# First norm of a two-layer trunk step: the modulation of channel blocks 4 and 5, and of 6 and 7, computed side by side

## The chip, the cores and the metric

The kernel runs on one core of a Trainium2 chip. The metric is the device time of one execution in microseconds (us). The kernel before took 1227.86 us, the median of three runs (1227.62 to 1229.47).

A core has five engines that run side by side, each through its own queue in order: TensorE (PE in the profile, with its weight loads as PEld), VectorE (DVE), ScalarE (ACT), GpSimd (POOL) and SyncE (SP), which here only issues DMA transfers. They wait for each other by semaphores. TensorE writes its results into PSUM, a memory of 8 banks, from which DVE and ACT read.

## The reference, cut to what matters

Two layers, run on 128 context tokens and 256 latent tokens, 1024 channels. Each layer begins with a norm whose scale and shift come from a conditioning vector by a matrix product (the "modulation"), and one wide input projection of the normed tokens:

```python
mod = jnp.einsum('bd,de->be', jax.nn.silu(cond), p['w_ada']) + p['b_ada']
sh1, sc1, g1, sh2, sc2, g2 = jnp.split(mod[:, None, :], 6, axis=-1)
h = _rms(x, p['g_norm1']) * (1 + sc1) + sh1
u = h @ p['w_in']
...
x = x + g1 * (merged @ p['w_out'])
h2 = _rms(x, p['g_norm2']) * (1 + sc2) + sh2
x = x + g2 * _conv_ffn(h2, p['w_up'], p['conv_w'], p['conv_b'], p['w_down'])
```

`_rms` divides by the root of the mean square over the channels. Between these lines stand four token mixers (pooling, differential attention, a Fourier transform, latent attention). The change touches only how `sh1`, `sc1` and the first part of `h @ p['w_in']` of layer 0 are put in order.

## The kernel before

Tokens lie along the free dimension (384 columns), channels along the 128 partitions, so the 1024 channels are 8 blocks (`KD = 8`), and a product of 128 output channels is a sum over 8 channel blocks. Each product is done in three matmuls of 128 x 384, with the weight and the activation each split into a high and a low part (high x high, high x low, low x high). ACT makes the high parts, DVE the low parts.

At the start of layer 0 everything is new: conditioning, modulation weights, tokens and projection weights arrive by DMA while the first norm is being computed. The kernel therefore goes block by block over the input channels. For channel block j there are these pieces of work, with their names in the code:

- **The loads** (SP, L473 and L475): `start_ada`, 1024 KB of modulation weights for block j, and `start_raw`, 448 KB of projection weights (seven output blocks of 128). SP issues them in the order of j, the two of a block one behind the other. There are six buffers for `start_ada` (`START_ADA = 6`), so those of blocks 6 and 7 are issued once the modulation of block 0 and of block 1 is done.
- **The modulation**, `start_modulate(j)` (PE, L1492), below **M j**: 32 small matmuls. The stationary operand is the conditioning vector padded to 32 columns, so each matmul fills 32 of the 128 columns of the array, in four strips; the result is 64 columns wide and lands in PSUM bank 7, in columns of its own for each block. In the profile a group of these has 64 records.
- **The norm**, `start_norm(j)` (DVE, L1066 to L1088): it waits until M j is done, reads it out of bank 7 with a transpose (L1066, which counts up the semaphore `start_read`), adds the bias (L1073), forms the scale (L1077), and scales the tokens (L1082, two instructions). It then makes the low part of the projection weights of this block (L1058, `start_low`), and, when ACT has made the high part of the normed block (`act_hi`, L658), the low part (L1088, two instructions).
- **ACT**, in its own order: the high part of the projection weights of block j (`start_hi`), then `act_hi` of block j, then `start_hi` of block j + 1.
- **The products**, `start_products(j)` (PE, L1503, L1507, L1508), below **P j**: 21 matmuls of 128 x 384 into banks 0 to 6, seven high x high first (L1503), then seven pairs of (high weight x low activation, L1507) and (low weight x high activation, L1508). P j waits for `start_hi` and `act_hi` of block j, and behind its first seven for the low parts.

PE's order in the kernel before is M0, M1, P0, M2, P1, M3, P2, M4, P3, M5, P4, M6, P5, M7, P6, P7: the modulation of block j + 2 stands between P j and P j + 1. Two semaphores keep PE and DVE apart in bank 7, which both use: M j waits until DVE has read the modulation of block j - 1 (`start_read >= j`, L1487), and DVE waits for M j as a whole (`ada_done >= 2 * (j + 1)`, L1065).

Behind P7 comes the first dense unit of the rest of the projection (L1435 to L1437), whose weights come through the general stream (`w_raw`, four slots), and then the rest of the layer. SP's queue behind the starting loads: four units of the stream, parameters, caches, constants; then two loads of modulation rows (`ada<-ada_rows`, L446), which wait for M7; then loads that wait for P7.

The loop that the change rewrites, and the two waits:

```python
if j >= 1:
    pe.wait_ge(start_read, j)
...
start_modulate(0)
start_modulate(1)
for j in range(KD):
    start_products(j)
    if j + 2 < KD:
        start_modulate(j + 2)
```

Of the kernel before, what the change touches and what calls it, by code (L numbers as in the profile page):

```python
# [25 lines left out]
KD = D // P  # L26
# [30 lines left out]
ADA = 48  # L57
HEAD = 16
START_ADA = 6
WARM = 11  # L60


# [110 lines left out]
def program(nc, stream, start_w, ada_w, ada_rows, start_ada, params, caches, consts, time_consts, x_in, cond,  # L173
            y_out, k_out, v_out, ckv_out, krope_out):
    ctx = ExitStack()
    with ctx:
        def tile(name, width, offset, dt=F32, parts=P):

            offset = -(-offset // 32) * 32
            return nc.alloc_sbuf_tensor_at(name, [parts, width], dt, offset=offset), offset + 4 * width  # L180

        def sem(name):
            return ctx.enter_context(nc.semaphore(name))
# [8 lines left out]
        late_t, _ = tile("gated_late", KD * TOK, o)  # L192
# [62 lines left out]
        brl_t, _ = tile("branch_lo", 8 * TOK, first_at, F32R)  # L255
# [12 lines left out]
        headb_t, _ = tile("ada_head_b", HOLE_LOW * UNIT, alo_at)  # L268
# [19 lines left out]
        start_ada_buf = [tile("start_ada0", 2 * UNIT, ada_at)[0]]  # L288
        o = rt_end - 4 * 2 * LAT - 4 * 2 * UNIT * (START_ADA - 1)
        assert o >= val_at  # L290
        for n in range(1, START_ADA):
            t, o = tile(f"start_ada{n}", 2 * UNIT, o)
# [40 lines left out]
        def pc(name, a=0, b=None, p0=0, p1=P):  # L333
            lo, hi = PCOL[name]
            return par[p0:p1, lo + a:(hi if b is None else lo + b)]

        def cc(name, p0=0, p1=P, a=0, b=None):
            lo, hi = CCOL[name]
            return cn[p0:p1, lo + a:(hi if b is None else lo + b)]
# [26 lines left out]
        shift_ready, gate2_ready = sem("shift_ready"), sem("gate2_ready")  # L366
        start_ada_loaded = [sem(f"start_ada_loaded{n}") for n in range(START_ADA)]
        start_w_loaded = [sem(f"start_w_loaded{j}") for j in range(KD)]
# [9 lines left out]
        hi_ready, lo_ready, unit_done, ada_done = sem("hi_ready"), sem("lo_ready"), sem("unit_done"), sem("ada_done")  # L378
# [37 lines left out]
        def _(sp):  # L416
# [53 lines left out]
            for j in range(KD):  # L470
                if j >= START_ADA:
                    sp.wait_ge(ada_done, 2 * (j - START_ADA + 1))
                sp.dma_start(start_ada_buf[j % START_ADA][:, :], start_ada[j:j + 1, :, :].rearrange("a p n -> (a p) n")  # L473
                             ).then_inc(start_ada_loaded[j % START_ADA], 16)
# [462 lines left out]
        def _(dve):  # L937
# [32 lines left out]
            for l in range(DEPTH):  # L970
# [84 lines left out]
                def start_low(j):  # L1055

                    dve.wait_ge(start_w_hi, j + 1)
                    V.tensor_tensor(start_lo[j][:, :], start_raw[j][:, :], start_hi[j][:, :].bitcast(F32), ALU.subtract  # L1058
                                    ).then_inc(start_w_lo, 1)

                def start_norm(j):

                    c0 = j * 2 * STRIP
                    turned_block = rt_t[:, c0:c0 + 2 * STRIP].rearrange("p (b c) -> p b c", c=STRIP)
                    dve.wait_ge(ada_done, 2 * (j + 1))  # L1065
                    turn = V.transpose(rt_t[:, c0:c0 + 2 * STRIP], bank[7][:, c0:c0 + 2 * STRIP])  # L1066
                    if j < KD - 1:
                        turn.then_inc(start_read, 1)
                        dve.wait_ge(start_read, j + 1)
                    else:  # L1070
                        turn.then_inc(mod_read, 2)
                        dve.wait_ge(mod_read, FROM + 2)
                    V.tensor_tensor(mod[:, j:2 * KD:KD, :], turned_block[:, :, 0:2],  # L1073
                                    pc("b_ada", 0, 2 * KD)[:, j:2 * KD:KD].unsqueeze(2).to_broadcast([P, 2, 2]), ALU.add
                                    ).then_inc(start_shift, 1)
                    dve.wait_ge(start_shift, j + 1)
                    own(V.scalar_tensor_tensor(sc1[:, j:j + 1, :], mod[:, KD + j:KD + j + 1, :], 1.0,  # L1077
                                               pc("g1", j, j + 1).unsqueeze(2).to_broadcast([P, 1, 2]), ALU.add, ALU.mult))
                    own.wait()
                    dve.wait_ge(rstd_ready, 1)  # L1080
                    for a, b, c in RANGES:
                        ins = V.scalar_tensor_tensor(wide[:, j, a:b], x[:, j, a:b], sc1[:, j, c:c + 1], rsn[:, a:b],  # L1082
                                                     ALU.mult, ALU.mult)
                    ins.then_inc(norm_full, 1)
                    start_low(j)
                    dve.wait_ge(norm_hi, j + 1)
                    for a, b, c in RANGES:
                        ins = V.scalar_tensor_tensor(alo[:, j, a:b], wide[:, j, a:b], mod[:, j, c:c + 1],  # L1088
                                                     ahi[:, j, a:b].bitcast(F32), ALU.add, ALU.subtract)
                    ins.then_inc(norm_lo, 1)  # L1090
# [293 lines left out]
        def _(pe):  # L1384
# [30 lines left out]
            def hole_units():  # L1415

                pe.wait_ge(mod_read, FROM + READ_AT[1, 3])
                for n in range(KD):
                    if n % 4 == 0:
                        pe.wait_ge(hole_ada_loaded[n // 4], 64)  # L1420
                    modulate(hole[n], HOLE_ADA + n)

            pe.wait_ge(ones_loaded, 16)
            for l in range(DEPTH):
# [47 lines left out]
                def start_squares():  # L1472

                    for _ in range(WARM):
                        T.matmul(bank[6][:, 0:P], cc("ones"), cc("ones"), start=True, stop=True)
                    for h in range(2):
                        pe.wait_ge(start_sq_sum, h + 1)
                        for k in (4 * h, 4 * h + 1):
                            ins = T.matmul(bank[4][:, 0:TOK], cc("ones"), wide[:, k, :], start=k == 0, stop=k == 5)
                    ins.then_inc(ss_done, 1)  # L1480

                def start_modulate(j):

                    w = start_ada_buf[j % START_ADA]
                    pe.wait_ge(start_ada_loaded[j % START_ADA], 16 * (j // START_ADA + 1))
                    if j >= 1:
                        pe.wait_ge(start_read, j)  # L1487
                    n = 2 * STRIP
                    for k in range(KD):
                        for strip in range(4):  # L1490
                            p0, c = STRIP * strip, (k * 4 + strip) * n
                            ins = T.matmul(bank[7][p0:p0 + STRIP, j * n:(j + 1) * n], conds[:, k, :], w[:, c:c + n],  # L1492
                                           start=k == 0, stop=k == KD - 1)
                    ins.then_inc(ada_done, 2)

                def start_products(j):

                    outs = [bank[u][:, 0:TOK] for u in range(SKIP)]
                    cols = [slice(u * P, (u + 1) * P) for u in range(SKIP)]
                    pe.wait_ge(start_w_hi, j + 1)  # L1500
                    pe.wait_ge(norm_hi, j + 1)
                    for u in range(SKIP):
                        T.matmul(outs[u], start_hi[j][:, cols[u]], HI[j], start=j == 0, stop=False)  # L1503
                    pe.wait_ge(start_w_lo, j + 1)
                    pe.wait_ge(norm_lo, j + 1)
                    for u in range(SKIP):
                        T.matmul(outs[u], start_hi[j][:, cols[u]], LO[j], start=False, stop=False)  # L1507
                        ins = T.matmul(outs[u], start_lo[j][:, cols[u]], HI[j], start=False, stop=j == KD - 1)  # L1508
                        if j == KD - 1:
                            ins.then_inc(unit_done, 1)  # L1510

                if l == 0:
                    start_squares()
                    pe.wait_ge(cond_ready, 1)
                    start_modulate(0)
                    start_modulate(1)
                    for j in range(KD):
                        start_products(j)
                        if j + 2 < KD:
                            start_modulate(j + 2)  # L1520
                else:
                    square_sums(0)
                    hole_units()
                    group(0, (0, 1, 2), HI, LO, lambda k: pe.wait_ge(norm_lo, l * 2 * KD + k + 1))
# [463 lines left out]
```

## Time and profile before

| | |
|---|---|
| median of 3 runs | 1227.86 us (1227.62 to 1229.47) |
| the profiled execution's own time | 1227.43 us |
| its span (first to last instruction) | 1225.5 us |
| PE busy in it | 1209.1 us (99%) |
| DVE, ACT, POOL busy | 909.8, 574.4, 140.4 us |
| mean granted clock of TensorE | 0.999 |
| DMA | 198.82 MB, 162 GB/s over the span |

A timeline row gives start, length, engine, line, operation, output and inputs; `x7` is the number of instructions drawn together in the row, and the bracket at its end is how long the engine had been idle and what ended that. Matmul records are longer than their spacing, since they are pipelined: what one costs is read from the starts. "us to landing" of a DMA counts from its issue.

### The profile page before, as it was taken

How to read it: one execution, taken by the hardware profiler on the slowest of the kernel's cores; microseconds unless marked ns; L12 is line 12 of the kernel's file. 1: busy time of each engine (PE TensorE's matmuls, PEld its weight loads, DVE VectorE, ACT ScalarE, POOL GpSimd, SP SyncE). 2: the span in 40 equal slices, each digit the busy share in tenths (PEclk: the TensorE clock that was granted, in tenths of full speed). 3: DMA queues.
4: the chain of work that ended last, by engine and by line, in shares of the span. 5: the costliest groups of instructions: out<-in, count | busy, mean ns of one | idle time of the engine just before them, and what ended most of it. 6: DMA issues, size and time to landing. Idle time of an engine off the chain costs nothing.

```text
span 1225.5 us, 19777 instructions
## 1 busy us (share of the span) xinstructions
PE 1209.1 (99%) x7816; PEld 1150.7 (94%) x7816; DVE 909.8 (74%) x1671; ACT 574.4 (47%) x949; POOL 140.4 (11%) x109
## 2 busy tenths in 40 slices
PE   7999999999999999999999999999999999999999
PEld 6987999989989999999989889999998999999998
DVE  5588877848679999987787865765596977877432
ACT  3445565543265445443354446656335654554321
POOL 0222000007310000000115210000281000000000
PEclk9999999999999999999999999999999999999999
DMA  9853333544644444459664522222245334334343
GB/s 371 323 182 123 137 121 116 171 143 155 237 176 146 165 155 166 153 191 345 217 238 169 187 81 101 93 100 99 99 165 206 121 121 134 125 122 137 132 142 122
DMA packets 53532, 198.82 MB, mean 162 GB/s; under 512 B 6784, under 2 KB 7200, under 8 KB 51904
## 3 DMA queue, kind: packets, MB, share of 16 engines
q1 hardware_dynamic: 53120, 196.86, 46.0%
q8 instruction: 63, 1.03, 0.3%
q0 software_dynamic: 320, 0.69, 0.1%
q14 instruction: 29, 0.24, 0.1%
HBM read 195.25 MB, written 2.27 MB: 161 GB/s over the span
## 4 chain that ended last, share of the span: by engine, by line
PE 91%; DVE 4%; issue 2%; DMA 2%; ACT 1%; SPq 0%; DVEq 0%; ACTq 0%
PE bank L1435 26%; PE bank L1437 26%; PE bank L1436 26%; PE bank L1734 1%; DVE w_lo L976 1%; DMA start_ada<-start_ada 1%; PE bank L1714 1%; PE bank L1503 1%; PE bank L1508 1%; PE bank L1704 1%; PE bank L1507 1%; ACT w_hi L658 1%; DVE gated_late L1295 1%; PE bank L1689 1%; PE bank L1492 1%
## 5 line engine op out<-in xcount | busy, mean ns | idle before, releaser
L1435 PE MATMUL bank<-act_hi,w_hi 128*128 128x384 f32 x1368 | 465.0, 340 | 0.7 <-DVE act_lo L1051 0.3
L1437 PE MATMUL bank<-act_hi,w_lo 128*128 128x384 f32 x1368 | 457.8, 335 | 0.0
L1436 PE MATMUL bank<-act_lo,w_hi 128*128 128x384 f32 x1336 | 446.6, 334 | 0.0
L976 DVE TENSOR_TENSOR w_lo<-w_raw,w_hi 128x1024 fp32r<-128x1024 f32 x251 | 318.3, 1270 | 117.8 <-ACT w_hi L658 117.2
L658 ACT ACTIVATE w_hi<-w_raw 128x1024 fp32r<-128x1024 f32 x251 | 264.2, 1053 | 165.1 <-DMA w_raw<-stream 165.0
L1435 PEld LDWEIGHTS bank<-act_hi,w_hi 128*128 128x128 f32 x1368 | 257.1, 188 | 10.7 <-issue 6.5
L1437 PEld LDWEIGHTS bank<-act_hi,w_lo 128*128 128x128 f32 x1368 | 256.8, 188 | 0.0
L1436 PEld LDWEIGHTS bank<-act_lo,w_hi 128*128 128x128 f32 x1336 | 251.0, 188 | 0.6
L1437 PE MATMUL bank<-mlp_hi,w_lo 128*128 128x384 f32 x352 | 118.3, 336 | 0.0
L1435 PE MATMUL bank<-mlp_hi,w_hi 128*128 128x384 f32 x352 | 118.3, 336 | 0.0
L1436 PE MATMUL bank<-mlp_lo,w_hi 128*128 128x384 f32 x352 | 118.3, 336 | 0.0
L1341 DVE SCALAR_TENSOR_TENSOR mlp_tmp<-bank,params,mlp_tmp 128x127 f32<-128x127 f32 (+1 forms) x176 | 64.7, 409 | 38.0 <-ACT mlp_tmp L658 38.0
L658 ACT ACTIVATE mlp_tmp<-bank,params 128x384 f32<-128x384 f32 x88 | 54.2, 667 | 81.3 <-PE bank L1437 81.3
L1345 DVE SCALAR_TENSOR_TENSOR mlp_tmp<-bank,params,mlp_tmp 128x127 f32<-128x127 f32 (+1 forms) x176 | 65.2, 412 | 3.1
L1437 PEld LDWEIGHTS bank<-mlp_hi,w_lo 128*128 128x128 f32 x352 | 66.2, 188 | 0.0
L1435 PEld LDWEIGHTS bank<-mlp_hi,w_hi 128*128 128x128 f32 x352 | 66.2, 188 | 0.0
L1436 PEld LDWEIGHTS bank<-mlp_lo,w_hi 128*128 128x128 f32 x352 | 66.2, 188 | 0.0
L1229 DVE TENSOR_REDUCE small<-bank 128x1 f32<-128x384 f32 (+1 forms) x72 | 31.3, 463 | 40.8 <-PE bank L1705 15.6
L1007 DVE SCALAR_TENSOR_TENSOR row_products<-ada,cond_spread 128x1024 f32<-128x1024 f32 x48 | 61.0, 1270 | 0.6 <-DMA ada<-ada_rows 0.4
L658 ACT ACTIVATE gates_b<-bank 128x384 f32<-128x384 f32 x48 | 23.6, 492 | 67.6 <-PE bank L1437 67.3
L1007 DVE SCALAR_TENSOR_TENSOR row_products_mix<-ada,cond_spread_mix 128x1024 f32<-128x1024 f32 x38 | 52.1, 1372 | 0.2
L649 POOL TENSOR_TENSOR wide<-wide 128x768 f32<-128x768 f32 x8 | 17.3, 2158 | 274.9 <-DVE wide L1295 274.9
(246 smaller groups left out, 1590.1 us busy)
## 6 DMA issues: line engine op xcount, KB each, us to landing
w_raw<-stream SPq DMA_DIRECT2D x251, 512.0 KB, 3.3
ada<-ada_rows SPq DMA_DIRECT2D x48, 512.0 KB, 4.3
start_ada<-start_ada SPq DMA_DIRECT2D x8, 1024.0 KB, 18.5
ada_norm<-ada_w SPq DMA_DIRECT2D x16, 512.0 KB, 5.9
ada<-ada_w SPq DMA_DIRECT2D x8, 512.0 KB, 5.5
start_raw<-start_w SPq DMA_DIRECT2D x8, 448.0 KB, 19.1
ada_head_a<-ada_w SPq DMA_DIRECT2D x5, 512.0 KB, 6.7
cond_spread_mix<-cond_rows SPq DMA_DIRECT2D x2, 1024.0 KB, 8.2
```

The lines of the kernel that those rows point to most:

```text
L649: own(nc.gpsimd.tensor_tensor(g[:, 0:2, :], g[:, 0:2, :], g[:, 2:4, :], ALU.add))
L658: return nc.scalar.activation(out, in_, func, **kw)
L976: V.tensor_tensor(wlo[s][:, :], raw[s][:, :], whi[s][:, :].bitcast(F32), ALU.subtract).then_inc(lo_ready, 1)
L1007: V.scalar_tensor_tensor(out[:, :], ada[b % 2][:, :], 1.0, tile[:, t, :], ALU.mult, ALU.mult, accum_out=mod[:, at, t:t + 1]).then_inc(rows ...
L1229: own(V.reduce_max(small[:, c + m:c + m + 1], bank[score_bank(i, m)][:, 0:n], AX))
L1295: V.scalar_tensor_tensor(gated[d % GATED][:, n, :], gates[n * KD + d], 1.0, bank[branch_bank[4 * d + n]][:, 0:TOK], ALU.add, ALU.mult).the ...
L1341: own(V.scalar_tensor_tensor(f[:, m, a + 1:e], b[:, a:e - 1], before, f[:, m, a + 1:e], ALU.mult, ALU.add))
L1345: ins = V.scalar_tensor_tensor(f[:, m, a:e - 1], b[:, a + 1:e], behind, f[:, m, a:e - 1], ALU.mult, ALU.add)
L1435: T.matmul(out, wb[s][0][:, w, :], hi[k], start=first and k == 0, stop=False)
L1436: T.matmul(out, wb[s][0][:, w, :], lo[k], start=False, stop=False)
L1437: ins = T.matmul(out, wb[s][1][:, w, :], hi[k], start=False, stop=last and k == n - 1)
L1492: ins = T.matmul(bank[7][p0:p0 + STRIP, j * n:(j + 1) * n], conds[:, k, :], w[:, c:c + n], start=k == 0, stop=k == KD - 1)
```

## The change

PE's loop is now driven by a table of groups. Blocks 1, 2 and 3 are groups of one, blocks 4 and 5 are one group, and 6 and 7 another. PE first makes the modulations of a group, and then the products of the blocks one before them. `START_LAST` gives for each block the last block of its group. M5 and M7 no longer wait for a read by DVE; DVE reads block 4 only when M5 is done too, and block 6 only when M7 is done, so that PE never writes to bank 7 while DVE reads it.

```diff
 START_ADA = 6
+START_GROUPS = ((0,), (1,), (2,), (3,), (4, 5), (6, 7))
+START_LAST = [group[-1] for group in START_GROUPS for _ in group]
...
-                    dve.wait_ge(ada_done, 2 * (j + 1))
+                    dve.wait_ge(ada_done, 2 * (START_LAST[j] + 1))
                     turn = V.transpose(rt_t[:, c0:c0 + 2 * STRIP], bank[7][:, c0:c0 + 2 * STRIP])
...
-                    if j >= 1:
+                    if j >= 1 and START_LAST[j - 1] != START_LAST[j]:
                         pe.wait_ge(start_read, j)
...
                     start_modulate(0)
-                    start_modulate(1)
-                    for j in range(KD):
-                        start_products(j)
-                        if j + 2 < KD:
-                            start_modulate(j + 2)
+                    for together in START_GROUPS[1:]:
+                        for j in together:
+                            start_modulate(j)
+                        for j in together:
+                            start_products(j - 1)
+                    start_products(KD - 1)
```

PE's order becomes M0, M1, P0, M2, P1, M3, P2, M4, M5, P3, P4, M6, M7, P5, P6, P7. The order of instructions on DVE, ACT, POOL and SP stays as it was.

This is PE's queue before, from the end of P2 to the begin of P4. The numbers are buffers: `start_ada_148` is block 4's modulation weights and `start_ada_149` block 5's; `start_hi_128`, `_131` and `_134` are the projection weights of blocks 2, 3 and 4.

```order
L1507 MATMUL bank<-act_lo,start_hi_128 128x384
L1508 MATMUL bank<-act_hi,start_lo_127 128x384
L1492 MATMUL bank<-start_ada_148,cond_silu 32x64 x32
L1503 MATMUL bank<-act_hi,start_hi_131 128x384 x7
...
L1507 MATMUL bank<-act_lo,start_hi_131 128x384
L1508 MATMUL bank<-act_hi,start_lo_130 128x384
L1492 MATMUL bank<-start_ada_149,cond_silu 32x64 x32
L1503 MATMUL bank<-act_hi,start_hi_134 128x384 x7
```

And the same stretch of the changed kernel (its lines are two higher here):

```order
L1509 MATMUL bank<-act_lo,start_hi_128 128x384
L1510 MATMUL bank<-act_hi,start_lo_127 128x384
L1494 MATMUL bank<-start_ada_148,cond_silu 32x64 x32
L1494 MATMUL bank<-start_ada_149,cond_silu 32x64 x32
L1505 MATMUL bank<-act_hi,start_hi_131 128x384 x7
...
L1509 MATMUL bank<-act_lo,start_hi_131 128x384
L1510 MATMUL bank<-act_hi,start_lo_130 128x384
L1505 MATMUL bank<-act_hi,start_hi_134 128x384 x7
```

M5 has moved ahead of the 21 matmuls of P3, and P4 follows P3 directly. The same happens around P5. Before, from the end of P4 to P6 (`start_ada_144` and `_145` are the buffers of blocks 6 and 7, `start_hi_137` and `_140` the weights of blocks 5 and 6):

```order
L1508 MATMUL bank<-act_hi,start_lo_133 128x384
L1492 MATMUL bank<-start_ada_144,cond_silu 32x64 x32
L1503 MATMUL bank<-act_hi,start_hi_137 128x384 x7
...
L1508 MATMUL bank<-act_hi,start_lo_136 128x384
L1492 MATMUL bank<-start_ada_145,cond_silu 32x64 x32
L1503 MATMUL bank<-act_hi,start_hi_140 128x384 x7
```

And in the changed kernel:

```order
L1510 MATMUL bank<-act_hi,start_lo_133 128x384
L1494 MATMUL bank<-start_ada_144,cond_silu 32x64 x32
L1494 MATMUL bank<-start_ada_145,cond_silu 32x64 x32
L1505 MATMUL bank<-act_hi,start_hi_137 128x384 x7
...
L1510 MATMUL bank<-act_hi,start_lo_136 128x384
L1505 MATMUL bank<-act_hi,start_hi_140 128x384 x7
```

M7 has moved ahead of P5, and P6 follows P5 directly. On PE two of the six places where a modulation stands between products are gone; on the other engines nothing moves, only what they wait for.

## Rows read from the trace of the kernel before

**Rows 1.** The page, busy time of each engine: us (share of the span) xinstructions.

```profile
PE 1209.1 (99%) x7816; PEld 1150.7 (94%) x7816; DVE 909.8 (74%) x1671; ACT 574.4 (47%) x949; POOL 140.4 (11%) x109
```

**Rows 2.** Waits of PE, whole span: waiting <- waited for: us, times, longest.

```profile
PE bank L1435 <- DVE w_lo L976: 2.7, 3, 2.0
PE bank L1557 <- ACT rstd L658: 2.5, 2, 2.2
PE bank L1492 <- DMA start_ada<-start_ada: 2.0, 2, 1.6
```

**Rows 3.** Timeline of PE: M1, M2, M4, P3, M5, P4, P6, P7, first dense unit.

```profile
14.86 1.10 PE L1492 MATMUL bank<-start_ada,cond_silu 128*32 128x64 f32 x64 [1.64 <-DMA start_ada<-start_ada]
20.19 1.10 PE L1492 MATMUL bank<-start_ada,cond_silu 128*32 128x64 f32 x64 [0.39 <-DMA start_ada<-start_ada]
29.96 1.10 PE L1492 MATMUL bank<-start_ada,cond_silu 128*32 128x64 f32 x64
30.99 1.48 PE L1503 MATMUL bank<-act_hi,start_hi 128*128 128x384 f32 x7
...
34.83 1.10 PE L1492 MATMUL bank<-start_ada,cond_silu 128*32 128x64 f32 x64
35.87 1.48 PE L1503 MATMUL bank<-act_hi,start_hi 128*128 128x384 f32 x7
...
45.61 1.48 PE L1503 MATMUL bank<-act_hi,start_hi 128*128 128x384 f32 x7
49.36 1.38 PE L1503 MATMUL bank<-act_hi,start_hi 128*128 128x384 f32 x7
53.00 0.34 PE L1435 MATMUL bank<-act_hi,w_hi 128*128 128x384 f32 x1
```

**Rows 4.** The modulations' matmuls, whole span: count, ns min/median/max, first and last start.

```profile
L1492 PE MATMUL bank<-start_ada,cond_silu x512: 219/219/243, 12.1 to 45.5; 128*32 128x64 f32 x171
```

**Rows 5.** Timeline of DVE and ACT, norm of block 4.

```profile
31.13 0.25 DVE L1066 STREAM_TRANSPOSE rope_tmp<-bank 128x64 f32<-128x64 f32 x1 [1.77 <-PE bank L1492]
32.47 1.08 DVE L1058 TENSOR_TENSOR start_lo<-start_raw,start_hi 128x896 fp32r<-128x896 f32 x1
32.65 0.80 ACT L658 ACTIVATE act_hi<-wide,mod 128x128 fp32r<-128x128 f32 x2 [3.23 <-DVE wide L1082]
33.49 0.75 DVE L1088 SCALAR_TENSOR_TENSOR act_lo<-wide,mod,act_hi 128x128 fp32r<-128x128 f32 x2
```

**Rows 6.** Loads of blocks 4, 5 and 7: issue on SP, then us to landing.

```profile
7.45 0.43 SPq L473 DMA_DIRECT2D start_ada<-start_ada  x1
8.40 0.84 SPq L473 DMA_DIRECT2D start_ada<-start_ada  x1
16.67 1.61 SPq L473 DMA_DIRECT2D start_ada<-start_ada  x1
start_ada<-start_ada SPq DMA_DIRECT2D x1, 1024.0 KB, 19.8
start_ada<-start_ada SPq DMA_DIRECT2D x1, 1024.0 KB, 22.4
start_ada<-start_ada SPq DMA_DIRECT2D x1, 1024.0 KB, 21.4
```

**Rows 7.** Timeline: the two row loads behind M7, and ACT's first stream units.

```profile
45.74 1.14 SPq L446 DMA_DIRECT2D ada<-ada_rows  x2
48.05 2.94 ACT L658 ACTIVATE w_hi<-w_raw 128x1024 fp32r<-128x1024 f32 x3
```

**Rows 8.** Timeline of ACT and PE between 64 and 74 us.

```profile
64.55 0.60 ACT L658 ACTIVATE val<-bank 128x512 f32<-128x512 f32 x1 [5.75 <-PE bank L1540]
73.33 0.61 PE L1557 MATMUL bank<-rstd,consts 32*128 32x384 f32 x4 [2.20 <-ACT rstd L658]
```

**Rows 9.** Stretches: us, busy (x) of PE, PEld, DVE, ACT, POOL, granted clock, DMA share, GB/s.

```profile
308.00:312.00 4.00, 2.14 (x10) 2.17 (x11) 4.00 (x6) 0.53 (x1) 2.85 (x3) 0.89 0.34 122
312.00:316.00 4.00, 4.00 (x17) 4.00 (x17) 4.00 (x3) 0.29 (x1) 3.60 (x2) 0.68 0.80 283
```

## The prediction

> **What bounds the kernel now.** I read the page first. PE is busy 99% of the span [rows 1], so a change counts only where it alters PE's time: an instruction less, a stall less or a wait more. Then the waits of PE alone [rows 2]: the largest are 2.7, 2.5 and 2.0 us, spread over the program, so there is no large wait to be won, and the third of them is the place of the change, the modulations that waited for their weights. Third, the timeline of PE in the first 53 us [rows 3]. The reader is to see where the loads pace PE and where they no longer do: M1 at 14.86 and M2 at 20.19 are released by a DMA; from then on no row of PE up to the first dense unit carries a bracket, so PE works through its queue without a visible wait. From M2 on this stretch is bound by PE itself, in steps of 34.83 - 29.96 = 4.87 us for one modulation and one block of products.
>
> **What a modulation between products costs.** P7 stands between two pieces of full-width work and takes 53.00 - 49.36 = 3.64 us. P6 comes from a modulation and goes into products: 49.36 - 45.61 = 3.75 us. P3 comes from a modulation and goes into one: 34.83 - 30.99 = 3.84 us [rows 3]. Entering products from a modulation thus costs 0.11 us, and leaving them for one 0.09. The modulation takes 30.99 - 29.96 = 1.03 us from its first matmul to the first product. But its group of 64 records is 1.10 us long and one record of it lasts 0.219 [rows 4], so the last one starts 0.88 us after the first; at that spacing (0.88 / 63 = 0.014) a following modulation could start after 0.89. The remaining 0.14 us is again the step from strips to full width. Put between products, a modulation has 0.20 + 0.14 = 0.34 us of such steps beside 0.89 of its own.
>
> **What the change removes.** M5 no longer stands between P3 and P4, nor M7 between P5 and P6. The same 32 matmuls run directly behind M4 and M6. No instruction is added or dropped. The boundary M4 to M5 (and M6 to M7) has no row in this trace. From below: it costs nothing, each pair saves 0.34 us, the two 0.68. From above: the boundary also carries a wait (for the weights), and if it pays the 0.14 us of the modulation's end and a new entry of 0.09, a pair saves 0.11, the two 0.22. Below nothing I exclude, since 0.89 us is already the bare spacing of the records. The nearest row of a boundary between like work is P6 to P7, whose waits are met and which costs nothing: P7 has the 3.64 us that 21 matmuls take at 0.173 each. I take nothing for the boundary: minus 0.68 us.
>
> [...]
>
> **What the change adds: waits.** There are three.
>
> First, M5 is reached earlier, at 29.96 + 0.89 = 30.85 us instead of 34.83, and needs the modulation weights of block 5. They were issued at 8.40 and landed 22.4 us later, at 30.80 [rows 6]. That is 0.05 us of slack where there were 4.03. In this execution the wait is zero; it is the one step of the change that hangs on a DMA, and it has a rival of its own below. For M7 the margin is wide: reached at about 40.25, its weights landed at 16.67 + 21.4 = 38.07; those of block 6 are ahead of them in the same queue. Queued behind a waiting M5 is all of PE: P3, whose data is ready, and everything after.
>
> Second, DVE reads block 4 only after M5. In the trace the transpose starts 31.13 - 29.96 = 1.17 us after its modulation starts, `act_hi` of the block is done (32.65 + 0.80) - 31.13 = 2.32 us after the transpose, and the low part (33.49 + 0.75) - 31.13 = 3.11 us after it [rows 3, 5]. Now the transpose comes at 30.85 + 1.17 = 32.02, 0.89 late against before; `act_hi` is there at 34.34, the low part at 35.13. P4 is due at 30.85 + 1.03 + 3.75 = 35.63, and needs the low part 1.2 us later (seven matmuls of 0.173), at 36.84. Slack 1.29 and 1.71 us: P3, which now lies between, hides the whole chain. Both times run from the same M5, so a late M5 doesn't eat this slack. M7, block 6 and P6 are the same sum, with the same slack.
>
> Third, M6 waits until DVE has read block 5. That read follows the low part of block 4 directly, at 35.13, and M6 is due at 35.63 + 3.64 + 0.09 = 39.36: 4 us of slack. DVE's work on a block (3.11 us) is less than PE's (3.64), so the queue doesn't grow.
>
> **What moves with it.** P7 now starts at 48.67 and the first dense unit at 52.31, 0.69 (rounding) before 53.00. The two row loads that wait for M7 are issued some 4.3 us earlier than 45.74 [rows 7]. They queue behind everything that the next products need, and ahead of loads that wait for P7, so they delay nothing. ACT's first high parts of the stream followed `act_hi` of block 7 directly at 48.05 [rows 7]; block 7's norm no longer waits for its own modulation (transpose at 45.61 - 1.03 + 1.17 = 45.75) but follows block 6's low part (40.25 + 1.17 + 3.11 = 44.53), so they come about 1.2 us earlier, and don't become the bound.
>
> **Does the gain survive to the end?** The next wait of PE is 2.20 us at 73.33, for a reciprocal root on ACT. It ends a chain that began with PE (ACT's `val` at 64.55 waited 5.75 us for PE's L1540) [rows 8]. The loads of that stretch are themselves issued on signals of PE, so the whole chain shifts with it. PE's other waits, on DVE in the two merges [rows 2], are of the same kind.
>
> **Sum.** The profiled execution: 1227.43 - 0.68 = 1226.75 us (span 1225.5 to about 1224.8, 1.9 us around it as before). The median of the runs shown is 0.43 above the profiled one; I forecast against it: 1227.86 - 0.68 = 1227.18, rounded 1227.2.
>
> **The rivals.**
> - *Half the gain.* The boundary between two modulations costs its upper bound or part of it: 0.22 to 0.40 us are saved, 1227.5 to 1227.6. For it: the waiting instruction is there, and at 14 ns per record a modulation gives it little cover. Against it: P6 to P7.
> - *Slower, by a late transfer.* M5 waits for its weights, and all of PE with it. The landings of blocks 4 and 5 are at 27.25 and 30.80, a step of 3.55 us [rows 6], but from block 1 (14.86) to block 2 (20.19) it was 5.33 [rows 3]. If a step like this falls ahead of block 5, it lands 1.78 late, M5 starts 1.73 later than in my sum, and the result is 1.05 us slower than before: 1228.9. It decides from 0.73 us of lateness on; before, M5 had 4.03 us of cover. Against it: in this trace the steps behind block 2 were even.
> - *Given back later.* Some wait of PE behind the first dense unit is not paced by PE but by a transfer, and takes up the 0.7: 1227.9. For it: three of PE's waits are on DVE, whose own inputs come by DMA. Against it: the chain to 73.33 [rows 8], and a PE without waits in most of the program.
> [...]
>
> **How the numbers follow.** My forecast (0.4 to 0.7 saved) gets 0.55, half the gain 0.20, the late transfer 0.10, given back 0.08, the clock 0.07, half of it to each side. The range is 1225.9 to 1229.2: down to the gain with most of a clock fall gone, up to the two slower rivals and some of the spread that the runs before show. 0.2% (2.5 us), about what a measurement of this kernel can tell from no change, is more than any of these terms but one: faster than 1225.4 needs my gain and the clock's gift together, 0.02; slower than 1230.3 the late transfer and a second clock fall, 0.03; so 0.95 for no difference.
>
> **What would show it right or wrong.** Right: M5 0.89 to 0.9 us behind M4 without a DMA wait of note, P3 to P4 and P5 to P6 3.75 us apart, the first dense unit near 52.3. Half the gain: M4 to M5 1.0 us or more. Late transfer: a bracket at M5 that names the DMA. Second chain: a wait before P4 or P6 for `act_hi` or the low part. Given back: the first dense unit is 0.7 earlier, and a later row of PE isn't. I am wrong as a whole if the first dense unit comes at 53.00 or later without a DMA wait before it.

## The result and the profile after

| | before | changed |
|---|---|---|
| median | 1227.74 us (22 runs, 1225.41 to 1231.10) | 1230.09 us (22 runs, 1227.38 to 1232.62) |
| ratio | | 1.0016, 95% interval 1.0010 to 1.0023 |
| profiled execution | 1227.43 us, span 1225.5 | 1230.85 us, span 1229.1 |
| M2's start to the first dense unit, in the trace | 53.00 - 20.19 = 32.81 us | 54.40 - 19.66 = 34.74 us |

The change makes the kernel about 2 us slower, where I had forecast 0.68 faster. The last line of the table is the measure used below: M2 waits for a transfer in both kernels, so what lies before it doesn't count; from there to the first dense unit is the stretch of the change. It moved by 1.93 us.

The page of the changed kernel: its busy time, where the answer to [rows 1] is the same work in a longer span, and one of its DMA queues, of the kind "instruction", which matters below.

```profile
PE 1210.2 (98%) x7816; PEld 1151.8 (94%) x7816; DVE 909.1 (74%) x1671; ACT 574.7 (47%) x949; POOL 140.4 (11%) x109
```

```profile
q8 instruction: 63, 1.03, 0.3%
```

The waits of PE over its span, against [rows 2]. The first three are as before (to 0.1 us); the fourth is new, and "issue" means that PE waited for nothing that the profile shows.

```profile
PE bank L1437 <- DVE w_lo L978: 2.6, 2, 2.0
PE bank L1560 <- ACT rstd L660: 2.5, 2, 2.2
PE bank L1494 <- DMA start_ada<-start_ada: 2.0, 2, 1.6
PE bank L1494 <- issue: 2.0, 2, 1.4
```

The timeline of PE, against [rows 3]: M1, M2, M4 with M5, P3, P4, M6 with M7, P5, P6, P7, first dense unit.

```profile
14.36 1.10 PE L1494 MATMUL bank<-start_ada,cond_silu 128*32 128x64 f32 x64 [1.64 <-DMA start_ada<-start_ada]
...
19.66 1.10 PE L1494 MATMUL bank<-start_ada,cond_silu 128*32 128x64 f32 x64 [0.36 <-DMA start_ada<-start_ada]
...
29.41 2.04 PE L1494 MATMUL bank<-start_ada,cond_silu 128*32 128x64 f32 x125
32.86 0.30 PE L1494 MATMUL bank<-start_ada,cond_silu 128*32 128x64 f32 x3 [1.41 <-issue]
33.10 1.49 PE L1505 MATMUL bank<-act_hi,start_hi 128*128 128x384 f32 x7
36.85 1.38 PE L1505 MATMUL bank<-act_hi,start_hi 128*128 128x384 f32 x7
40.58 1.32 PE L1494 MATMUL bank<-start_ada,cond_silu 128*32 128x64 f32 x80
42.48 0.88 PE L1494 MATMUL bank<-start_ada,cond_silu 128*32 128x64 f32 x48 [0.58 <-issue]
43.29 1.49 PE L1505 MATMUL bank<-act_hi,start_hi 128*128 128x384 f32 x7
47.07 1.38 PE L1505 MATMUL bank<-act_hi,start_hi 128*128 128x384 f32 x7
50.73 1.39 PE L1505 MATMUL bank<-act_hi,start_hi 128*128 128x384 f32 x7
54.40 0.35 PE L1437 MATMUL bank<-act_hi,w_hi 128*128 128x384 f32 x1
```

M4 and M5 run through without a break between them, as forecast, but stop after 125 of their 128 records; M6 and M7 stop after 80. The gaps are in the middle of a modulation, where the program has no wait at all. Counted from the start at which the next record was due (0.015 us behind the one before), 1.61 and 0.78 us are lost.

DVE and ACT on block 4, against [rows 5]; the second chain is as forecast. `act_hi` is done at 35.53, P4 starts at 36.85: 1.32 us of slack.

```profile
33.20 0.25 DVE L1068 STREAM_TRANSPOSE rope_tmp<-bank 128x64 f32<-128x64 f32 x1 [4.40 <-PE bank L1494]
34.73 0.80 ACT L660 ACTIVATE act_hi<-wide,mod 128x128 fp32r<-128x128 f32 x2 [5.86 <-DVE wide L1084]
35.56 0.75 DVE L1090 SCALAR_TENSOR_TENSOR act_lo<-wide,mod,act_hi 128x128 fp32r<-128x128 f32 x2
```

The load of block 5's modulation weights, against [rows 6], its issue on the timeline and its landing in the DMA view: it landed at 8.34 + 22.0 = 30.34. M5 was due at 29.41 + 0.89 = 30.30, and its first record, in the middle of the row x125 above, starts at 30.37, so this wait took under 0.1 us.

```profile
8.34 0.43 SPq L475 DMA_DIRECT2D start_ada<-start_ada  x1
```

```profile
start_ada<-start_ada SPq DMA_DIRECT2D x1, 1024.0 KB, 22.0
```

The two row loads and the first stream units, against [rows 7], and PE's wait for the reciprocal root, against [rows 8]; neither is a new bound.

```profile
43.41 0.81 SPq L448 DMA_DIRECT2D ada<-ada_rows  x2
48.67 2.94 ACT L660 ACTIVATE w_hi<-w_raw 128x1024 fp32r<-128x1024 f32 x3
74.77 1.34 PE L1560 MATMUL bank<-rstd,consts 32*128 32x384 f32 x8 [2.22 <-ACT rstd L660]
```

Stretches of the changed kernel, against [rows 9] (the last but two number is the granted clock):

```profile
75.00:80.00 5.00, 5.00 (x24) 4.04 (x21) 4.96 (x8) 1.56 (x3) 0.00 (x0) 0.66 0.52 191
308.00:312.00 4.00, 2.82 (x15) 2.21 (x13) 4.00 (x5) 1.47 (x2) 2.94 (x2) 1.00 0.35 111
312.00:316.00 4.00, 2.61 (x10) 2.64 (x11) 4.00 (x6) 0.52 (x1) 2.85 (x3) 0.76 0.22 82
```

In this execution the clock fell once more than in the profiled one of before, behind the wait at 74.77: (1 - 0.66) x 5 = 1.7 us. With the 1.93 us above, and 0.53 us less since the changed one was ahead at M2, that makes 3.1 of the spans' 3.6 us. The fall need not be the change's doing: the kernel before has a clock as low in part of its runs. Run by run on one chip (the last experiment), 9 of 21 runs before and 7 of 11 changed had a mean clock of 0.997. Those averaged 1229.11 and 1231.03 us: at the same clock the two kernels are 1.92 us apart, close to the 1.93 us of the timeline (1.86 in the profile of that experiment). The other clock values have one to seven runs a side, and give 1.4 to 2.3 us.

### The profile page after: what moved, and what is told of

It reads as the page before. It is cut to its first block, busy times and chain, and to the rows that moved or that the text cites. A ratio compares the mean times of both kernels' runs of the same rounds, so it can differ in the third digit from the quotient of the medians.

```text
span 1229.1 us, 19775 instructions
## 1 busy us (share of the span) xinstructions
PE 1210.2 (98%) x7816; PEld 1151.8 (94%) x7816; DVE 909.1 (74%) x1671; ACT 574.7 (47%) x949; POOL 140.4 (11%) x109
## 3 DMA queue, kind: packets, MB, share of 16 engines
q8 instruction: 63, 1.03, 0.3%
## 4 chain that ended last, share of the span: by engine, by line
PE 91%; DVE 4%; issue 2%; DMA 2%; ACT 1%; SPq 0%; DVEq 0%; ACTq 0%
PE bank L1437 26%; PE bank L1439 26%; PE bank L1438 26%; PE bank L1737 1%; DVE w_lo L978 1%; PE bank L1717 1%; DMA start_ada<-start_ada 1%; PE bank L1505 1%; PE bank L1510 1%; PE bank L1509 1%; PE bank L1707 1%; DVE gated_late L1297 1%; ACT w_hi L660 1%; PE bank L1692 1%; PE bank L1494 1%
```

## The experiments

The theory that came from the gaps: the two places are 3 records of M5, P3, P4 and 80 records of M6 and M7 apart. A record stands for a weight load and a matmul, so that is 6 + 84 + 160 = 250 instructions, and 6 more with those that only wait: 256. Queue 8 moved 63 packets of 16 KB; PE's 2 x 7816 instructions and the 445 that only wait in its program, divided by 63, are 255 to a packet. So PE's code comes in packets of 256 instructions, and a gap could be PE at the end of one with the next still under way (theory F).

Where the packets of queue 8 start can be found by narrowing a window of the DMA view. In the changed kernel those in question start within these two windows, 30.4 to 30.8 and 39.8 to 40.2 us; by narrowing further, at 30.54 and 39.99.

```profile
q8 instruction: 1, 0.02, 17.2%
```

```profile
q8 instruction: 1, 0.02, 17.3%
```

PE went on at 32.86 and 42.48, 2.33 and 2.49 us after. The rival is theory Q: TensorE's queue or sequencer can't supply two modulations in a row, wherever their code lies.

**Code moved by 120 instructions.**

```diff
+def pad(n):
+    for _ in range(n):
+        pe.wait_ge(ones_loaded, 16)
 def start_squares():
+    pad(48)
...
+    pad(64)     # behind the warm-up
...
 start_modulate(0)
+pad(56)
...
+    if j == 2:
+        pad(72)
```

> The changed kernel with 240 waits on a semaphore that is already met put into TensorE's program at the start (48 before the warm-up matmuls, 64 behind them, 56 behind M0, 72 between P0 and M2); two waits share an instruction, so all later code of TensorE lies 120 instructions further on. Theory F (code fetch): the two stalls of the changed kernel, 1.6 us near the end of M5 and 0.8 us in M7, stand 250 to 256 instructions apart, and the profile's queue 8 moves 16 KB packets of about 256 of TensorE's instructions each; TensorE stalls where it crosses into a packet that is still under way, which happens only if it has run through some 176 instructions in less than about 2.5 us, as it does when two modulations (256 instructions, 2.06 us) follow each other. 120 instructions later the packet ends fall at the middle of M4 and of M6, behind dense products that take 87 ns per instruction: no stall at all. M4's start to P3's start 1.9 to 2.1 us, M2's start to the first dense unit 32.1 to 32.3 us (32.81 before, 34.74 in the changed kernel), the time 0.5 to 0.7 us below before. Theory Q (TensorE's own queue or its sequencer can't supply matmuls of 14 ns for as long as two modulations): the stalls depend on the order of work, not on where the code lies, and stay at 1.6 and 0.8 us; M2 to the dense unit 34.7 us, the time 1.3 to 2.4 us above before. Theory D (M5's weights land late): same as Q, 34.7 us.

That two waits share an instruction is counted in the traces: the first line of this run's page has 19895 instructions, that of the changed kernel 19775, and TensorE's records that only wait are 565 against 445, so 240 waits are 120 instructions. The 176 in theory F was my estimate and no run shows it as a limit; by the count over TensorE's records, 94 and 164 instructions were still to go to the packet's end when the packets of 30.54 and 39.99 us started in the changed kernel.

The same in the kernel before:

> Control: the kernel before with the same 240 waits at the same places. Both theories: the waits stand where TensorE waits for data anyway or runs behind its queue, so nothing changes: M2's start to the first dense unit 32.8 us, time within 0.3 us of before. If the waits cost something, it is seen here ahead of M2. Theory F adds: no boundary between packets can stall this order, because between any two modulations stand 21 matmuls of 174 ns.

Here the page counts 19897 instructions against 19777 in before, again 120 for the 240 waits.

The changed kernel with its code moved, M4 with M5, P3, M6 with M7, P5:

```profile
33.93 2.27 PE L1503 MATMUL bank<-start_ada,cond_silu 128*32 128x64 f32 x128
36.12 1.48 PE L1514 MATMUL bank<-act_hi,start_hi 128*128 128x384 f32 x7
...
43.61 1.99 PE L1503 MATMUL bank<-start_ada,cond_silu 128*32 128x64 f32 x128
45.53 1.48 PE L1514 MATMUL bank<-act_hi,start_hi 128*128 128x384 f32 x7
```

Both gaps are gone. M6 to P5 takes 1.92 us (2.71 before the move), M4 to P3 2.19 (3.69). The 0.27 us more than 1.92 are a remnant of the first gap, too short for a bracket: record by record in the trace, the one behind the 65th of M4 and M5 comes 0.25 us after it, 2.48 us after the start of a code packet. So the packet's end lay there, at the start of M5, and not in the middle of M4 as the expectation says. M2 to the first dense unit is 56.56 - 24.16 = 32.40 us, 0.1 above what was expected, and 57.36 - 24.55 = 32.81 in the control, exactly as without the waits. Theory Q, by which the gaps stay, is out. The part on the total time failed: the waits themselves cost about 4.4 us ahead of M2 (PE's first matmul came at 5.96 us), so the ratios to before are 1.0036 (1.0024 to 1.0049) and, for the control, 1.0050 (1.0036 to 1.0064).

**Code moved by 32 instructions** (`pad(32)` before and behind the warm-up; 19807 instructions on the page, 32 more than the 19775 of the changed kernel).

> The changed kernel with 64 met waits (32 instructions) put around the warm-up matmuls. Theory F (code fetch): the end of the code packet moves 32 instructions, so 16 records, earlier in the work: the stall in M4 and M5 comes after about 109 of their 128 records instead of 125, and is about as long (1.2 to 1.8 us of gap). The second packet end falls at the boundary of M6 to M7; its fetch starts earlier in P4 by 32 x 87 ns, so there is no stall in M6 and M7. Theory Q (TensorE's queue or sequencer runs dry): the gap stays after 125 records, and the second one after 80.

```profile
29.39 1.88 PE L1503 MATMUL bank<-start_ada,cond_silu 128*32 128x64 f32 x109
32.64 0.53 PE L1503 MATMUL bank<-start_ada,cond_silu 128*32 128x64 f32 x19 [1.37 <-issue]
...
40.58 2.11 PE L1503 MATMUL bank<-start_ada,cond_silu 128*32 128x64 f32 x128
```

The gap moved by 16 records to exactly the 109th. The second pair has no bracket; 0.11 us are lost in it, at its 64th record, where the packet's end was expected. M2 to the dense unit is 53.65 - 19.58 = 34.07 us. One run, 1228.83 us.

**One pair alone.** `START_GROUPS` with `(4, 5), (6,), (7,)`, and with `(4,), (5,), (6, 7)`.

> Only M4 and M5 made together; M6 and M7 stand between products as before. Theory F: the code up to P4 lies as in the changed kernel, so the stall of 1.6 us near the end of M5 (after 125 of 128 records) stays. The next packet end falls some 30 instructions into P5: no stall. M2 to the first dense unit 32.81 - 0.34 + 1.6 = 34.1 us, the time 1.3 us above before. Theory Q: the same for this pair.

```profile
29.45 1.10 PE L1494 MATMUL bank<-start_ada,cond_silu 128*32 128x64 f32 x64
30.81 1.09 PE L1494 MATMUL bank<-start_ada,cond_silu 128*32 128x64 f32 x61 [0.27 <-DMA start_ada<-start_ada]
33.08 0.30 PE L1494 MATMUL bank<-start_ada,cond_silu 128*32 128x64 f32 x3 [1.18 <-issue]
```

The gap came after the same 125 records. M5 also waited for its weights in this run: 0.27 us idle, and 0.47 behind its due start, against 1.38 at the gap counted the same way. The late transfer of the prediction exists, at a third of the price. M2 to the dense unit is 54.15 - 19.70 = 34.45 us; ratio 1.0006 (0.9997 to 1.0015), that is -0.4 to +1.8 us, which holds the 1.64 us of the timeline and also nothing.

> Only M6 and M7 made together; M4 and M5 as before. Theory F: the packet end behind block 5 falls at about record 19 of M5, with P3 close before it: no stall; the next falls at about record 15 of M7 (after some 80 of the 128 records of M6 and M7), as in the changed kernel: a stall of 0.6 to 0.8 us. M2 to the first dense unit 32.81 - 0.34 + 0.78 = 33.25 us, the time 0.4 us above before. Theory Q: two modulations in a row stall as they do at M4 and M5 if only the order counts: 1.6 us, 34.1 us; at least it doesn't say why the second pair stalled half as long.

```profile
38.71 2.13 PE L1494 MATMUL bank<-start_ada,cond_silu 128*32 128x64 f32 x128
40.77 1.49 PE L1505 MATMUL bank<-act_hi,start_hi 128*128 128x384 f32 x7
```

A miss in size: 2.06 us for the pair where 1.92 is free of gaps, so 0.14 lost and not 0.79. They are lost in one place, behind the 80th record. M2 to the dense unit is 51.88 - 19.22 = 32.66 us, ratio 0.9999 (0.9990 to 1.0008). The packet had started at 37.41, with more of P4 still to run than in the changed kernel, and PE reached the packet's end at about 39.9, 2.5 us behind its start: just in time. Here the packet started 1.30 us ahead of M6 (37.41 against 38.71), in the changed kernel 0.59 (39.99 against 40.58). So the second gap is larger when the first pair is made too. That the first gap itself puts off the second packet is argued and not tested alone.

**Eight instructions of moving for that pair** (`pad(16)` before the warm-up; 19784 instructions on the page, 19776 without).

> M6 and M7 alone made together, with 16 met waits (8 instructions) ahead of the warm-up, where TensorE waits for its first data. In the run without these waits the pair lost 0.14 us (M6's start to P5's 2.06 us instead of 1.92): code packet at 37.41, packet end reached at 39.9. Theory F: 8 instructions less of P4 stand ahead of the fetch (0.7 us), so it is in time: M6 to P5 1.92 us, M2's start to the first dense unit 32.81 - 0.34 = 32.5 us, the time 0.3 us below before, which may be too little to be told from none. Theory Q: 2.06 us again, 32.66 us.

```profile
39.52 2.27 PE L1496 MATMUL bank<-start_ada,cond_silu 128*32 128x64 f32 x128
```

A miss in size once more: M6 to P5 took 41.73 - 39.52 = 2.21 us, M2 to the dense unit 32.81, ratio 1.0000 (0.9991 to 1.0009). The place did move as theory F has it: the loss is behind the 76th record, not the 80th, and four records are the eight instructions. But the packet started 2.78 us into P4 (38.47) instead of 2.54, later and not earlier. What starts a fetch is thus not known to within 8 instructions.

**Later transfers.** SyncE waits for M6 (`sp.wait_ge(ada_done, 2 * (KD - 1))`) ahead of the stream's loads.

> The changed kernel, but SyncE waits for M6 before it issues the four stream units and all that follows, so the DMA engines are empty from about 38.7 us (block 7's projection weights) until 41.5. The first code packet in question (start 30.5 us) still runs among full queues, the second (start 40.0) runs alone. Theory F with a fetch that waits behind data transfers: the stall in M5 stays at 1.6 us, that in M7 shrinks from 0.8 us to 0.3 or nothing. Theory F with a fetch of fixed length: both stay (2.3 to 2.5 us from packet start to the next matmul). The later loads cost nothing if they land before 48 us; if they don't, it shows behind P7.

M4 with M5 and M6 with M7, then the DMA queues (last number but one is the DMA share) of this run and of the changed kernel:

```profile
29.46 2.05 PE L1495 MATMUL bank<-start_ada,cond_silu 128*32 128x64 f32 x125
32.55 0.30 PE L1495 MATMUL bank<-start_ada,cond_silu 128*32 128x64 f32 x3 [1.03 <-issue]
...
40.39 1.99 PE L1495 MATMUL bank<-start_ada,cond_silu 128*32 128x64 f32 x128
```

```profile
36.00:38.00 2.00, 2.00 (x13) 2.00 (x12) 1.90 (x6) 0.63 (x3) 0.00 (x0) 1.00 0.36 138
```

```profile
36.00:38.00 2.00, 2.00 (x13) 2.00 (x12) 1.90 (x7) 0.63 (x2) 0.00 (x0) 1.00 1.02 408
```

The second gap is gone. The code packet started at 37.10 us, 0.5 us into P4, while the queues ran empty; in the changed kernel, with a DMA share of 1.02, it started 3.1 us into P4. Only the times of the loads were changed, so the start of the fetch hung on the data transfers: without them it came 2.6 us earlier in P4, in time. The gap in M5, whose packet still met full queues, shrank only to 32.55 - 31.31 = 1.24 us. M2 to the dense unit 33.70 us, ratio 1.0013 (1.0004 to 1.0023).

**A gap where none was.** 34 small matmuls between M0 and M1:

```diff
 start_modulate(0)
+for i in range(34):
+    p0 = STRIP * (i % 4)
+    T.matmul(bank[6][p0:p0 + STRIP, 0:2 * STRIP], conds[:, 0, :], conds_t[:, 0:2 * STRIP], start=True, stop=True)
```

> The changed kernel with 34 small matmuls of the modulation's form (32 columns by 64, 136 instructions, results unused, into bank 6) between M0 and M1, where TensorE waits 1.6 us for a transfer. Theory F: all packet ends fall 136 instructions earlier in the work: the stalls in M5 and M7 are gone or under 0.3 us, and a stall that no other kernel had appears at the end of M1 (a packet end falls after about 60 of its 64 records, behind 390 instructions without a dense product), 1 us or more. Theory Q: M4/M5 and M6/M7 stall as before, 1.6 and 0.8 us, and M1 too, since the small matmuls before it drain the queue.

M1, then both pairs:

```profile
14.52 1.09 PE L1494 MATMUL bank<-start_ada,cond_silu 128*32 128x64 f32 x60 [0.66 <-DMA start_ada<-start_ada]
18.48 0.30 PE L1494 MATMUL bank<-start_ada,cond_silu 128*32 128x64 f32 x4 [2.87 <-issue]
...
33.87 1.99 PE L1494 MATMUL bank<-start_ada,cond_silu 128*32 128x64 f32 x128
...
43.28 1.99 PE L1494 MATMUL bank<-start_ada,cond_silu 128*32 128x64 f32 x128
```

M1 stopped after exactly 60 records, and both pairs run free, 1.93 and 1.92 us. M2 to the dense unit is 56.23 - 24.13 = 32.10 us, 0.71 less than before: the gain of the prediction, with its size. The whole run, a single one, took 1231.57 us; the gap in M1 alone lost 3.1 us.

**Another pair.** `START_GROUPS = ((0,), (1,), (2,), (3,), (4,), (5, 6), (7,))`.

> Another pair: M5 and M6 made together, all other modulations between products as in the kernel before. Theory F: counted in TensorE's instructions, the packet ends lie 38 records into M5 (behind P3, fetch begun 4 us earlier) and in P5 (behind P4 and the first part of P5). Neither can stall, so this pair brings what the prediction gave a pair: M5's start to P4's start 1.92 us, M2's start to the first dense unit 32.81 - 0.34 = 32.47 us, the time 0.3 us below before. Theory Q (two modulations in a row run TensorE's queue dry, wherever the code lies): a stall of 0.8 to 1.6 us in M6, 33.3 to 34.1 us.

```profile
34.84 1.99 PE L1494 MATMUL bank<-start_ada,cond_silu 128*32 128x64 f32 x128
36.77 1.48 PE L1505 MATMUL bank<-act_hi,start_hi 128*128 128x384 f32 x7
```

No gap: 1.93 us, M2 to the dense unit 52.67 - 20.16 = 32.51 us. Ratio 0.9988 (0.9979 to 0.9997), 1227.02 us against 1227.88 on the same chip, so this version is a little faster than before and clearly faster than the changed kernel. Its timeline accounts for 0.3 us, and the interval reaches from 0.4 to 2.6: what the rest is, if it is real, stays open.

The same pair with 21 of the small matmuls between M0 and M1:

> The same pair M5, M6, with 21 small matmuls of the modulation's form (84 instructions, results unused) between M0 and M1, where TensorE waits 1.6 us for a transfer: 84 instructions more ahead of the pair, nothing else. Theory F: the packet end moves from P5 into the end of M6, after 124 of the 128 records of the pair, and the fetch begins in M5 or at the end of P3: a stall of 1.0 to 1.7 us there, M2 to the first dense unit 33.5 to 34.1 us. Theory Q: the same as the run without the small matmuls.

```profile
34.83 1.98 PE L1494 MATMUL bank<-start_ada,cond_silu 128*32 128x64 f32 x124
38.83 0.30 PE L1494 MATMUL bank<-start_ada,cond_silu 128*32 128x64 f32 x4 [2.02 <-issue]
```

The gap is at the forecast record, the 124th, and with 38.83 - 36.61 = 2.22 us larger than I had put it. M2 to the dense unit 55.06 - 20.17 = 34.89 us; one run, 1232.50 us. The order of the work around the pair is that of the run before; the place of its code differs, by 84 instructions that PE had run through 20 us earlier.

**The changed kernel again.**

> The changed kernel once more, to see whether its two stalls come again at the same record and to compare it with the others on one chip. Theory F: gaps after exactly 125 of the records of M4 and M5 and after 80 of those of M6 and M7, 1.0 to 1.5 and up to 0.8 us long, since the place is set by the code and the length by the transfers in the way. The time 1 to 2.4 us above before.

```profile
32.58 0.30 PE L1494 MATMUL bank<-start_ada,cond_silu 128*32 128x64 f32 x3 [1.31 <-issue]
42.22 0.88 PE L1494 MATMUL bank<-start_ada,cond_silu 128*32 128x64 f32 x48 [0.56 <-issue]
```

The gaps came after 125 and 80 records, 1.31 and 0.56 us idle; M2 to the dense unit 54.14 - 19.47 = 34.67 us. 1230.57 us against 1227.88, ratio 1.0018 (1.0009 to 1.0026).

## Why the prediction was wrong

- **The steps between strips and full width** held. A pair without a gap brings 0.30 us (the pair 5, 6), two bring 0.71 (the run with 34 small matmuls), against 0.34 and 0.68.
- **The boundary between two modulations** is where it failed. "Below nothing I exclude", and from above I had 0.22 us still saved: I bounded the instant between M4 and M5 by the nearest rows, and never asked whether PE gets its instructions at that rate. A modulation runs through 128 instructions in 1.03 us, products through 42 in 3.64. One modulation between two products leaves 3.6 us in every 4.9 in which few instructions are used and the next packet can come; two in a row use a whole packet in 2 us, less than the 2.3 to 2.7 us that passed between the start of a packet and the next matmul in every gap measured. The term is 1.61 + 0.78 us instead of 0; minus 0.68 that makes 1.7 of the 1.93 us. By the length of the pairs, which takes in M5's start and the first records behind a gap, it is (3.69 - 1.92) + (2.71 - 1.92) = 2.56 us, and 1.88 of the 1.93.
- **The three waits** held: M5 met its weights with a delay of 0.06 us (the slack of 0.05 in the prediction was below the 0.1 us to which the landing was read), the second chain had 1.32 us of slack for a forecast 1.29, M6 didn't wait for DVE.
- **The late transfer**, the rival that gave a slower kernel, was a transfer indeed, but of code and not of weights. Weights were late by more than 0.1 us in two runs: the pair 4, 5 alone (0.47 us) and the run with 32 instructions of moving (0.12).
- **Given back later** didn't happen: at the same clock the loss of the head is the loss of the whole.
- **The clock.** The range and the chances use a clock fall, whose size the traces show: (0.11 + 0.32) x 4 = 1.7 us in before [rows 9], and (1 - 0.66) x 5 = 1.7 us in the changed kernel at 75 to 80 us. From run to run the time moves with the mean clock, in before as in the others: on the chip of the last experiment the kernel before averaged 1227.54 us in 7 runs with a mean clock of 0.999 and 1229.11 in the 9 with 0.997. It is the spread, not the difference. No run shows what makes it fall, nor that a shift of PE takes a fall away or adds one.
- The chance of 0.95 for a change of less than 0.2% and the upper end of the range rested on a list of rivals in which only waits of the program stood. The measured 1230.09 us lies above the range's 1229.2.

Open stays what sets off a fetch. Each packet can be set against the moment at which PE enters the 256 instructions ahead of it. Later in the kernel before, one packet started 6.1 us ahead of that moment (94.25 against 100.40); in its first 50 us 1.3 to 3.6 us behind it; and behind the gap in M5 7.1 us (changed kernel), 7.2 (the pair 4, 5 alone) and 4.6 (later transfers). No run separates PE's lead, the full queues and the gap itself.

## What to carry to other kernels

Beside each engine's work ask for its instructions per microsecond: where, as here, 256 small instructions follow each other in 2 us while the DMA queues are full (a DMA share of 1.03 from 29.41 to 31.20 us in the changed kernel), the code itself is a transfer that can be late: 1.61 us at the first pair, 0.78 at the second. The sign is a gap marked "issue" in the middle of instructions that wait for nothing; its place moved one for one when instructions were added ahead of it (by 16 records for 32 instructions), and a control that moves only the code tells it from every cause that lies in the order of work. In this kernel one modulation at a time between products never stalled, and a pair that stalled at one place paid at the neighbouring one, as the pair 5, 6 did.

## What the runs showed of the hardware that was not expected

- TensorE's code came in packets of 256 instructions (63 packets of 16 KB). The place of a gap was forecast to the record in three kernels (after 109, 60 and 124 records). Counted over all of PE's instructions in the trace (weight loads, matmuls and waits), every gap of this kind and every loss of 0.1 to 0.3 us named above as a packet's end, in nine kernels, has 449, 962, 1217 or 1218 instructions ahead of it: to within one, whole multiples of 256 apart.
- From the start of a packet to the next matmul behind a gap passed 2.33 and 2.49 us in the changed kernel, and 2.35 to 2.72 in the six other runs with a gap; the packet itself took 1.1 to 1.3 us of them. A packet that started 3.1 us into P4 among full queues started 0.5 us into it when these ran empty. When a packet started, PE was by the same count never more than 301 instructions short of the first one in it.
- Two of the added waits were one instruction: 240 are 120 more on the page (19895 against 19775, and 19897 against 19777), 64 are 32 (19807 against 19775), 16 are 8 (19784 against 19776).
- A wait that is already met isn't free on TensorE's queue: in the runs with moved code their records start 0.106 us apart, and with 8, 16 and 24 of them ahead of it the first matmul came at 4.32, 5.13 and 5.96 us (6.02 in the control, 3.34 to 4.25 without).
